# A second fold of the even frequencies in the Hyena convolution, and an output projection that starts with the Hyena half

## The reference, cut to what matters

```
z, g1, g2 = u[..., :512], u[..., 512:1024], u[..., 1024:]
for o, gate in enumerate((g1, g2)):
    conv = irfft(rfft(z, n=2 * L, axis=1) * spec[:, o], n=2 * L, axis=1)[:, :L]
    z = gate * (conv + z * skip[o])
...
y_hy = _group_rms_norm(_hyena(hy, spec, hy_skip[l]), hy_norm_g[l], HYENA_GROUPS)
...
y_ml = _group_rms_norm(y_ml, ml_norm_g[l], MLSTM_HEADS)
mixed = concatenate([y_hy, y_ml], axis=-1)
h = h + mixed @ w_out[l]
```

## Time and profile before

| | us |
|---|---|
| median of 3 runs | 3569.22 (3565.95 to 3570.24) |
| the profiled execution | 3566.57 |
| span of its trace | 3564.8 |
| PE busy in the span | 3332.7 (93%) |
| `phase_convolve` and its end, by the trace | about 428 to 728 |
| the block of `phase_mix` | about 842 to 865 |

### The profile page before, as it was taken

The page is one execution under the profiler, slowest core; times in us unless marked ns, Lnnn a source line. Parts: engine busy times, 40 slices in busy tenths (PEclk is TensorE's granted clock), DMA queues, the critical chain, the costliest instruction groups (busy, mean ns, idle before and its releaser), DMA issues. The chain is left out here.

```text
span 3564.8 us, 40485 instructions
## 1 busy us (share of the span) xinstructions
PE 3332.7 (93%) x15544; PEld 2663.5 (75%) x15544; DVE 1758.4 (49%) x2739; ACT 1112.2 (31%) x2015; POOL 560.6 (16%) x378
## 2 busy tenths in 40 slices
PE   7999899976898899999999998988999899999998
PEld 5777688865786678888888776775567688888886
DVE  4415655565422446555544539789654332332434
ACT  4323344354322222111111433136674221211112
POOL 0002466722000001000001200000263200010010
PEclk9999999987999999999999999999999999999999
DMA  3232324412121113333321301123333121111111
GB/s 115 87 104 70 130 88 136 142 61 92 54 71 59 42 59 95 100 102 105 104 83 62 105 18 42 48 57 90 76 73 113 30 71 48 47 47 47 51 43 59
DMA packets 223644, 269.80 MB, mean 76 GB/s; under 512 B 17277, under 2 KB 150294, under 8 KB 221062
## 3 DMA queue, kind: packets, MB, share of 16 engines
q1 hardware_dynamic: 223496, 267.78, 24.4%
HBM read 219.16 MB, written 29.18 MB: 70 GB/s over the span
## 5 line engine op out<-in xcount | busy, mean ns | idle before, releaser
L193 PE MATMUL psum<-rounded,rounded 128*128 128x512 f32 (+2 forms) x3936 | 1537.7, 391 | 64.6 <-DVE rounded L222 51.6
L194 PE MATMUL psum<-rounded,rounded 128*128 128x512 f32 (+2 forms) x3936 | 1528.7, 388 | 0.0
L195 PE MATMUL psum<-rounded,rounded 128*128 128x512 f32 (+2 forms) x3936 | 1528.2, 388 | 0.0
L193 PEld LDWEIGHTS psum<-rounded,rounded 128*128 128x128 f32 x3936 | 746.6, 190 | 239.1 <-DVE rounded L222 56.8
L195 PEld LDWEIGHTS psum<-rounded,rounded 128*128 128x128 f32 x3936 | 746.1, 190 | 151.8
L194 PEld LDWEIGHTS psum<-rounded,rounded 128*128 128x128 f32 x3936 | 747.2, 190 | 148.9 <-issue 0.2
L3002 DVE TENSOR_TENSOR plain<-psum,plain 128x512 f32<-128x512 f32 x432 | 288.6, 688 | 110.4 <-PE psum L195 108.8
L3013 DVE TENSOR_TENSOR plain<-psum,plain 128x512 f32<-128x512 f32 x44 | 30.4, 692 | 425.1 <-ACT plain L2917 425.1
L3579 POOL TENSOR_TENSOR plain<-plain,plain 128x128 f32<-128x128 f32 (+3 forms) x64 | 97.3, 1530 | 563.4 <-ACT plain L3680 506.4
L3376 DVE TENSOR_SCALAR_CACHE_REDUCE plain<-plain,plain 128x384 bf16<-128x384 f32 (+2 forms) x204 | 181.8, 942 | 1.4
L2994 DVE TENSOR_TENSOR rounded<-plain,rounded 128x512 fp32r<-128x512 f32 x108 | 96.9, 897 | 166.0 <-ACT rounded L2906 165.9
(11 more groups left out here) (326 smaller groups left out, 3457.5 us busy)
## 6 DMA issues: line engine op xcount, KB each, us to landing
plain<-in_ff_w_dram SPq DMA_DIRECT2D x64, 512.0 KB, 5.4
plain<-in_w_ada_dram SPq DMA_DIRECT2D x96, 256.0 KB, 3.5
plain<-in_w_gu_dram SPq DMA_DIRECT2D x44, 512.0 KB, 5.0
plain<-in_w_in_dram SPq DMA_DIRECT2D x36, 512.0 KB, 4.0
rounded<-rounded SPq DMA_DIRECT2D x72, 256.0 KB, 3.4
plain<-in_c_fwd_dram SPq DMA_DIRECT2D x64, 256.0 KB, 2.6
plain<-in_w_down_dram SPq DMA_DIRECT2D x22, 512.0 KB, 3.7
fold<-plain SPq DMA_DIRECT2D x8, 1024.0 KB, 4.8
```

What stands on the lines that cost most here:

```text
L193: nc.tensor.matmul(out, wh, xh, start=first, stop=False)
L194: nc.tensor.matmul(out, wh, xl, start=False, stop=False)
L195: return nc.tensor.matmul(out, wl, xh, start=False, stop=last)
```

## The change

**Convolution.** The even frequencies of the signal are folded a second time, so that a transform over 512 folded tokens becomes two over 256; the odd ones share a second fold on the side of the tables. The filter's own transform keeps its size. A round now has 36 units: 16 for the filter (206 matmuls), 12 for the signal (166), 8 back (114), 486 in all, 972 for both rounds. Every signal unit of the first four frequency tiles feeds two banks; the tiles run in the order `SIGNAL_ORDER`, and tiles 4 and 6, and 5 and 7, are combined in pairs by DVE (`pair`) before they are rounded. The tokens are stored in strides of two (`TOKENS` when turned, `COLUMNS` when turned back). The row at token 512 no longer stands apart; in its place there are corrections on single rows, among them `fix_folds`, which waits for the folds and precedes their splitting. All of the gating (`near`, `far`) comes after the last bank.

**Projection.** `phase_mix` is gone. `MixNorm` runs inside `phase_rows_gemm_norm`: PE multiplies the first 512 rows of `w_out` (the Hyena half) while ACT and DVE norm the mLSTM half, and the transposes stand between these products at the places given by `TURNS`, through banks 6 and 7. The first piece of `w_out` is loaded and split inside `phase_mlstm`. POOL has no part in the norm any more.

Cut to its core:

```diff
+COLUMNS = ([(0, slice(0, 256, 2))], [(0, slice(512, 256, -2))], ...
+TOKENS = (slice(0, 256, 2), slice(256, 512, 2), slice(1, 256, 2), slice(257, 512, 2), ...
 # phase_conv_proj, PE, ACT, DVE
-last = nc.tensor.transpose(ps[...], tmp[m % 2][:, t * P:(t + 1) * P], core.ident)
+last = nc.tensor.transpose(ps[...], tmp[m % 2][:, TOKENS[t]], core.ident)
...
+SIGNAL_ORDER = (0, 1, 2, 3, 4, 6, 5, 7)
+SIGNAL_AT, INVERSE_AT, ROUND_UNITS = 16, 28, 36
-FOLD_ORDER = ((0, 1, 3, 2), (0, 2, 3, 1))
+FOLD_ORDER = ((0, 3, 1, 2), (0, 3, 2, 1))
+EVEN_COS, ODD_COS, ODD_SIN, EVEN_SIN = range(4)
+def signal_done(n):
+    return SIGNAL_AT + (n + 1 if n < 4 else 2 * n - 2)
...
+def signal_pe(core, pe, tables, zfold, quarter, R):
+    for n, j in enumerate(SIGNAL_ORDER):
+        if n < 4:
+            pe.wait_ge(R.sem("act_free"), R.at("act_free", n + 5))
+        else:
+            pe.wait_ge(R.sem("dve_done"), R.at("dve_done", n - 3))
+        if j < 4:
+            tables.products(pe, one, B + n, zfold, cos, True, j >= 2)
...
+            ins = tables.products(pe, two, B + n, zfold, sin, True, j != 0, block=2)
...
+        else:
+            u = B + 2 * n - 4
+            tables.products(pe, one, u, zfold, range(4, 8), True, True).then_inc(done, 1)
+            tables.products(pe, two, u + 1, zfold, range(0, 4), True, False)
+            mm3(nc, two, eighth[0:1, 0, :], ...).then_inc(done, 1)
+def inverse_pe(core, pe, tables, y, R):
+    for p in range(2):
+        for part in range(2):
+            n = 2 * p + part
+            pe.wait_ge(R.sem("dve_done"), R.at("dve_done", 5 + n))
+            pe.wait_ge(R.sem("y_lo"), R.at("y_lo", 4))
+            tables.products(pe, one, B + n, y, (src, src + 1), True, False)
...
+    pe.wait_ge(R.sem("y_lo"), R.at("y_lo", 6))
...
 # phase_convolve, ACT
 def fold_high(R, n):
     act.wait_ge(R.sem("fold%d" % n), R.at("fold%d" % n, 16))
+    if n >= 1:
+        act.wait_ge(R.sem("fold_fixed"), R.at("fold_fixed", 1))
...
+for n in range(4):
+    until(B + signal_done(n))
+    act.wait_ge(R.sem("pool_done"), R.at("pool_done", n + 1))
+    nc.scalar.activation(y.hi[:, n::TT, :], y.raw[:, n::TT, :], ACT.Copy).then_inc(R.sem("w_hi"), 1)
+for b in range(2):
+    until(B + signal_done(5 + 2 * b))
+    act.wait_ge(R.sem("paired"), R.at("paired", b + 1))
...
 # phase_convolve, POOL
-for u in range(B, B + UNITS + 4):
+for u in range(B, B + SIGNAL_AT + 3):
     tables.low(pool, u)
-for j in range(TT):
-    for u in (B + UNITS + 2 * j + 4, B + UNITS + 2 * j + 5):
-        tables.low(pool, u)
-    pool.wait_ge(R.sem("dve_done"), R.at("dve_done", j + 1))
+low = B + SIGNAL_AT + 3
+for n, j in enumerate(SIGNAL_ORDER):
+    while low < min(B + signal_done(n) + 3, B + INVERSE_AT):
+        tables.low(pool, low)
+        low += 1
+    pool.wait_ge(R.sem("dve_done"), R.at("dve_done", n + 1))
     # two operations on 128 x 512, then pool_done
-for u in range(B + 2 * UNITS + 4, B + ROUND):
+for u in range(low, B + ROUND_UNITS):
     tables.low(pool, u)
 # phase_convolve, DVE
+def fix_folds(R):
+    for n in range(1, 4):
+        dve.wait_ge(R.sem("fold%d" % n), R.at("fold%d" % n, 16))
     # two and then two operations on 1 x 512, then fold_fixed
 for R in rounds:
+    if R.o == 0:
+        fix_folds(R)
+        for n in range(4):
+            fold_low(R, n)
+    fold_signal(R)          # eight operations on 128 x 1024, four on one row
+    if R.o == 1:
+        fold_low(R, 2)
+        fold_low(R, 3)
...
+    for n, j in enumerate(SIGNAL_ORDER):
         # four products, dve_done
+        if 1 <= n <= 4:
+            low(n - 1)
+        if n == 6:
+            pair(0)
+    low(4)
+    pair(1)
+    low(5)
+    if R.o == 0:
+        fold_low(rounds[1], 0)
     # four times: wait for ACT's copy of one bank, add and subtract the other (terms)
+    if R.o == 0:
+        fix_folds(rounds[1])
+        fold_low(rounds[1], 1)
+    for p in range(2):
+        nc.vector.tensor_tensor(near, terms[:, p, 0:2, :], terms[:, p, 2:4, :], ALU.add)
+        chain(nc.vector.tensor_tensor(far, terms[:, p, 0:2, :], terms[:, p, 2:4, :], ALU.subtract))
+        if p == 0:
             # four operations on 1 x 512
+        for n, (made, t) in enumerate(((near, 2 * p), (far, 4 + 2 * p))):
+            nc.vector.tensor_tensor(made, made, gates[:, t:t + 2, :], ALU.mult).then_inc(...)
+            if R.o == 1:
                 # squares and reduce_sum on 128 x 1024
-def phase_mix(core, src, yht, mixed, scratch, ahead):
...
+class MixNorm:
+    TURNS = {(1, 5): (0, 1), (2, 2): (2,), (2, 5): (3,), (3, 2): (4,), (3, 5): (5, 6, 7)}
+    def scalar(self, act):
+        for j in range(4):
+            nc.scalar.activation(self.mixed.hi[:, j, :], self.yht[:, j, :], ACT.Copy).then_inc(S["v_hi"].sem, 1)
+            if j == 0:
+                nc.scalar.activation(self.rstd, self.ss, ACT.Sqrt, ...)
         # then mixed.hi of each turned tile
+    def vector(self, dve):
+        given(0)            # mixed.lo of a Hyena tile, 128 x 1024
+        nc.vector.reciprocal(self.rstd, self.rstd)
+        given(1); scaled(0); given(2); scaled(1); given(3)
+        for t in range(2, TT):
+            scaled(t)       # four scalar_tensor_tensor on 128 x 128
+            low(t - 2)
+        low(TT - 2); low(TT - 1)
+    def first_half(self, pe, weights):
+        tiles = [(k, t) for k in range(4) for t in range(6)] + [(k, t) for t in (6, 7) for k in range(4)]
         # mm3 for each (k, t); tile 6 starts only when z_lo is 8; turns where TURNS says
 # phase_mlstm
+sp.dma_start(piece.raw, w).then_inc(S["loaded0"].sem, 16)
+pool.wait_ge(S["w_hi"].sem, S["w_hi"].at(1))
+nc.gpsimd.tensor_tensor(piece.lo, piece.raw, piece.hi_raw, ALU.subtract).then_inc(S["w_lo"].sem, 1)
```

More of the change, by code:

```diff
@@ L73, in constants @@
+def constants():
+    fwd, sig, inv, order = transforms()
     p = np.arange(P)
@@ L993, in low, with products @@
         self.core.nc.gpsimd.tensor_tensor(w.lo, w.raw, w.hi_raw, ALU.subtract).then_inc(S["ft_lo"].sem, 1)
-    def products(self, pe, out, u, src, at, first, last):
+    def products(self, pe, out, u, src, tiles, first, last, block=0):
         nc, S, w = self.core.nc, self.core.sig, self.ring[u % 4]
         pe.wait_ge(S["ft_lo"].sem, S["ft_lo"].at(u + 1))
-        for k in range(4):
-            ins = mm3(nc, out, w.hi[:, k, :], w.lo[:, k, :], src.hi[:, at + k, :], src.lo[:, at + k, :], first and k == 0, last and k == 3)
+        for n, k in enumerate(tiles):
+            ins = mm3(nc, out, w.hi[:, block + n, :], w.lo[:, block + n, :], src.hi[:, k, :], src.lo[:, k, :], first and n == 0, last and n == len(tiles) - 1)
         return ins
@@ new lines, in _ @@
+                for p in range(2):
+                    for part in range(2):
+                        u = INVERSE_AT + 5 + 2 * p + part
+                        until(B + u)
+                        act.wait_ge(R.sem("aux_done"), R.at("aux_done", u))
+                        if p == 0:
+                            nc.scalar.activation(rows[part], ps[0:1, 2 * part + 1, :], ACT.Copy)
+                        nc.scalar.activation(kept_sums[:, p, part, :], ps[:, 4 * p + 2 * part, :], ACT.Copy).then_inc(R.sem("act_done"), 1)
@@ L2029, in _ @@
                             scaled(h, s)
+                    if h == NH and s == 0:
+                        act.wait_ge(S["loaded0"].sem, S["loaded0"].at(16))
+                        nc.scalar.activation(piece.hi, piece.raw, ACT.Copy).then_inc(S["w_hi"].sem, 1)
                     if h >= 1:
@@ L2189, in turn @@
                 norm.turn(pe, t)
-            for p in range(4):
+            if mix is not None:
+                mix.first_half(pe, ring[0])
+            for p in range(0 if mix is None else 1, 4):
                 c, kh = p // 2, p % 2
@@ L2212, in _ @@
         def _(act):
-            for p in range(4):
+            if mix is not None:
+                mix.scalar(act)
+            for p in range(0 if mix is None else 1, 4):
                 if modulated is not None:
@@ L2250, in _ @@
                 nc.vector.tensor_tensor(carried, norm.ss1[:, 0:TT], norm.ss1[:, TT:2 * TT], ALU.add).then_inc(S["row_first"].sem, 1)
-            for p in range(4):
+            if mix is not None:
+                mix.vector(dve)
+            for p in range(0 if mix is None else 1, 4):
                 if p == 0:
@@ L2299, in phase_rows_gemm_norm @@
     norm.close()
-    first.close()
+    if mix is None:
+        first.close()
+    else:
+        mix.close()
     if modulated is not None:
```

697 lines of the change are left out of this document (385 added, 312 removed).

## The result

The changed kernel takes 3627.2 us (median of 4 runs, 3623.0 to 3629.3); the kernel before, run beside it, 3567.6 (3564.5 to 3570.2). The ratio is 1.0166, 95% interval 1.0148 to 1.0184. The forecast was 3594, with 3622 as its upper end: right in its sign, less than half as large as what came (+27 against +60).

The account below looks back on a forecast made before the run. PE was taken as the bound, busy 93% of the span and full in the convolution. The terms summed to +24.8 us on the profiled 3566.57, giving 3591.4; with the median 2.6 above, 3594, range 3555 to 3622.

Parts of the forecast that it names:

- Matmuls, -65.4: Convolution: 288 fewer matmuls at 0.227 us each save 65.4 us, if PE has its operands in time.
- Waits of the lists: Signal part: PE waits for tables before units 21 to 23, 27 and 28; with clock restarts +53.6 us for both rounds.
- the ring: Signal part: POOL combines, ACT rounds y, then `high`, then POOL's `low`; 5.8 us a turn, 8.4 us of waits a round.
- The clock, 14.9 forecast in the convolution: Convolution: after PE stands still, its restart at 1.2 GHz costs 2.5 us each time.
- Between the rounds, +23.4: Round 1, after 110 matmuls: PE waits 20.9 us behind DVE's gating, folding and splits, plus 2.5 for the clock.
- Start, +8.4: Convolution's start: `fix_folds` waits for all folds ahead of the first split, so PE starts 8.4 us later.
- End, +18.5: After round 1's last matmul: DVE does all gating, squares and sums alone, 24.8 us where it was 6.4.
- Mix, -14.9: Output projection: PE multiplies the Hyena half while the mLSTM half is normed, saving 14.9 us by the 96th matmul.
- Projection of the inputs, +1.0: Projection of the inputs: added ACT and DVE operations lie under the next tile's 48 matmuls except for the last tile, +1.0 us.
- tables in time: Rival, signal part: the lists don't hold up the tables, the 53.6 us go, 3540 us or 3517; chance 0.17.
- the projection overlaps nothing: Rival, output projection: transposes wait for DVE at each place of `TURNS`, the 14.9 us gain shrinks to 0, 3609 us; chance 0.10.
- strided reading: Rival, projection of the inputs: the 96 strided transposes cost 12.5 us more where 0 was taken, 3607 us; chance 0.10.

Follow-up runs that it names:

- r7: Changed kernel with 16 of the convolution's 60 one-row matmuls given 128 rows, the added weights being zero: 3626.3 us, timed once.
- r1: Changed kernel with POOL's limit lifted, so tables 28 to 30 may get their low parts before the last frequency tile is combined: 3616.8 us.
- r2: Changed kernel with ACT and POOL both preparing one more table before waiting for a tile's result, POOL's limit before unit 28 kept: 3601.1 us.
- c1: Changed kernel with POOL's limit lifted and ACT alone one table further ahead, POOL staying three tables ahead: 3591.3 us.
- r4: Changed kernel with round 1's fold splits of blocks 1 to 3 made ahead of the gating, and the folded signal rounded later: 3614.8 us.
- r5: Changed kernel with DVE splitting fold block 0 ahead of `fix_folds` in round 0: 3620.5 us.
- r8: Kernel before with only the projection part of the change (`MixNorm`, early first piece of weights), convolution left old: 3554.3 us.
- r6: Changed kernel with DVE weighing a filter's first channel block before folding the filter ahead of it, in the projection of the inputs: 3608.7 us.

## Why the prediction was wrong in size and right in sign

- **Matmuls, -65.4.** 972 matmuls, as said. Mis-sized by 10.7: I priced every one at 0.227. One-row matmuls stand apart by 0.33 with each change between 128 rows and one (r7).
  The Trainium skill (TensorEngine Tiling (Array Packing), in the section on the tiling modes' key properties) says that changing the tiling mode drains TensorE. The section doesn't say that a matmul of one row among those of 128 is such a change. The rows show a price at each passage and none within a group, which would fit; whether a drain is the cause no run here shows.
- **Waits of the lists.** Before units 21 to 23 I said 8.4 us a round; 6.7 and 7.0 came. Before unit 27: 6.6, measured 6.1. Before unit 28: 6.8, measured 8.6. Four small ones of 0.6 to 2.6 (6.2 us in all) I hadn't seen. With the wait between the rounds: 64.5 forecast, 65.5 measured. The mechanisms are shown: r1 took away the wait before unit 28, r2 the one before unit 27, and c1 brought those of the ring from 6.7 and 7.0 us to 2.5 and 2.9.
- **The clock, 14.9 forecast in the convolution, 15.3 measured.** The sum is right, but that is in part luck: in r1, r4, r5 and r7 the waits went down or stayed and the loss at 1.2 GHz went up to 21 or 22. The gain of an edit can't be had from its wait alone, by 5 to 7 us.
- **Between the rounds, +23.4.** The wait was 16.2 us, not 20.9, and stood at the place said, after 110 matmuls. DVE's chain was right: with E the end of PE's inverse (604.8 us), DVE was through at E+42.6 (forecast E+44.5) and PE went on at E+46.1 (E+46). What was off is when PE arrived there: at E+30 and not E+25, by the wait of 2.6 in this stretch, 1.4 at 1.2 GHz and 1.1 for one-row matmuls. DVE was slowed early, as said: 2.29 us for an operation that took 1.21 after POOL's last `low` of this stretch, which ended at 625.5.

```profile
612.37 8.99 POOL L1071 TENSOR_TENSOR rounded<-plain,rounded 128x512 fp32r<-128x512 f32 x4 [5.56 <-ACT rounded L1066]
...
614.02 2.29 DVE L1479 TENSOR_TENSOR plain<-plain 128x1024 f32<-128x1024 f32 x1
...
626.52 1.21 DVE L1479 TENSOR_TENSOR plain<-plain 128x1024 f32<-128x1024 f32 x1
```

  I had PE wait for the bank; it waited for a `high` behind the same ACT writes, some 2 us longer. r4 shows that it was DVE's chain.
- **Start, +8.4.** 10.0 in this execution, 7.7 to 8.9 in the seven others with the same start; r5 shows the cause. **End, +18.5.** 17.9. **Mix, -14.9.** -13.2 in the trace, -13.3 in the median of r8. The 1.7 us are a second stretch at 1.2 GHz that I hadn't counted, behind the waits of the last turns: nine matmuls in 3.75 us from 937.09 on.
- **Projection of the inputs, +1.0.** This is the step that failed: +14.9 and 0.8. I wrote that the added operations "lie under the next tile's 48 matmuls". They lie ahead of `weigh` on DVE, and PE waits for `weigh`: it stands idle for 9.6 us before the matmuls with the taps, where it was 2.7. I had checked the cover of the tile loop and not the queue of the engine; r6 shows it with one turned pair of calls. (r6 moves all of `fold`, and part of it stood ahead of `weigh` before the change too: it shows the queue, not what the added operations alone cost.) The other 8 us of this execution are matmuls at 1.2 GHz, and they vary: in the eight kernels with this stage as in the changed one the same event lies between 430.7 and 436.1 us, so the stage costs 9.5 to 14.9.
- **Strided transposes, 0.** Eight took 1.04 us and 1.11 or so after; line 916's weight loads take 207 ns in the mean for 147, but that hardly shows in the starts. In all some 1 us of 12.5 possible: the rival was wrong.
  In the Trainium skill's note on cachelines (SBUF — State Buffer, in the section on the DMA port swizzle) the half by which a stride of two float32 is free holds to within this 1 us of the time, though the load itself got 60 ns longer.
- **After the mix, 0.** +8.3: 2.0 of it between 963 and 1000 us of the trace before, and 4.5 in the sparse attention, between 2496 and 2590 us there, which the change doesn't touch (the 100 us from its start have a granted clock of 0.91 for 0.97). From the 96th product to the end the thirteen kernels with the new mix took between 2675.5 and 2683.0 us, with the same code there and no relation to their edits; the kernel before took 2674.2. So up to 7.5 us is variation of this stretch, and the 1.3 by which all thirteen lie above the kernel before may be the change's own or not: there is one trace of before. What makes the stretch vary is not shown; I take it for the clock.

The misses add up: 14.7 (projection with its transposes) + 1.6 (start) + 12.3 (convolution, 10.7 of it the one-row matmuls) - 1.6 (end, group norm) + 1.7 (mix) + 8.3 (after the mix) = 37.0, within rounding the 61.7 less the 24.8 forecast. The queue of `weigh` is the largest, but not all of it: the one-row matmuls, which I priced like the others without a row for it, and the variation after the mix make up half. The rivals: "tables in time" was wrong from the first wait on; "the projection overlaps nothing" and "strided reading" too. The case I hadn't listed, an engine's queue in a stage I called covered, weighed most.

## What to carry to other kernels

A fold that saves matmuls is paid in operations of the other engines, and each is paid where its queue has an instruction behind it that PE waits for: go through every queue that gets an operation and ask what stands behind it, also in the stage that looks covered. When one list waits in a ring of engines, moving two of its lists by the same count moves the ring and leaves it closed; open it by letting the producer alone go ahead. And where PE was full before, price the waits by the order of the programs first, and the saved matmuls last: here 65 us of saved matmuls were worth, after all seams were mended, some 5 us that the intervals don't tell from nothing.

## What the runs showed of the hardware

- Each passage from 128 rows to one and back costs 0.2 us of PE in two distances of 0.33 instead of 0.227, 0.40 us for a group; four one-row matmuls in a row cost no more than two.
- A POOL operation of 1.29 us took 2.26 to 2.31 in three turns beside DVE's 128 x 1024 subtraction (c1), where 1.75 had been seen before. DVE's own started 0.1 us ahead of it each time and kept its 1.23. The other way round, DVE's 128 x 1024 operation took 2.29 instead of 1.21 beside POOL's `low`s.
- The time that PE's matmuls lose at 1.2 GHz varies with nothing in the code that would explain it: in the convolution it was 15.3 and 15.8 us in two kernels with the same code there, and 21.5 and 21.8 in two that differ in the order of one split (r5) or in 16 one-row matmuls (r7), with waits of 65.4 to 66.1 us in all four. The projection ahead of it ended within 5.4 us in eight kernels with the same code.
